# Two of TensorE's transpositions handed to DMA, and the opening's transfers in another order

## What is computed

```python
for l in range(DEPTH):                                   # 2 layers
    x = x + 0.5 * swiglu(rms_norm(x, ...), w_ffn1_in[l], w_ffn1_out[l])
    x = x + hybrid_mixer(rms_norm(x, ...), mem, ...)
    x = x + 0.5 * swiglu(rms_norm(x, ...), w_ffn2_in[l], w_ffn2_out[l])

# hybrid_mixer: four branches of width 512 over h, gated and summed
proj = h @ w_in
o_a = moba_attention(...)              # 8 heads of 64, rotary; causal softmax (one block of 256)
o_b = multiscale_pool(...)             # four running means, mixed by four 128x128 matrices
o_c = forgetting_attention(...)        # "fox": 8 heads of 64, causal softmax with a decay term
o_m = memory_cross_attention(...)      # 4 heads of 128; keys and values from mem
y = einsum('bsnc,ncd->bsnd', stack(o_a, o_b, o_c, o_m), w_branch)
return sum(sigmoid(gate_logits) * y) @ w_out
```

## Time and profile before

| | |
|---|---|
| Median of 3 runs | 1331.98 us (1331.53 to 1332.44) |
| The profiled execution's own time | 1332.22 us |
| Its span | 1330.3 us |
| PE busy | 1324.3 us, 100% of the span |
| DVE busy | 930.7 us, 70% |
| ACT busy | 681.0 us, 51% |
| POOL busy | 260.8 us, 20% |
| DMA, mean | 200 GB/s |

### The profile page before, as it was taken

The page is one execution under the profiler, slowest core; times in us unless marked ns, Lnnn a source line. Parts: engine busy times, 40 slices in busy tenths (PEclk is TensorE's granted clock), DMA queues, the critical chain, the costliest instruction groups (busy, mean ns, idle before and its releaser), DMA issues.

```text
span 1330.3 us, 15825 instructions
## 1 busy us (share of the span) xinstructions
PE 1324.3 (100%) x6140; PEld 1095.3 (82%) x6140; DVE 930.7 (70%) x1182; ACT 681.0 (51%) x952; POOL 260.8 (20%) x257
## 2 busy tenths in 40 slices
PE   9999999999999999999999999999999999999999
PEld 7888888888888888888888888888888888888887
DVE  5666777789897675666475664787999876665653
ACT  5444465554655455454355454556546545544442
POOL 0323312033120002333003230020522100033220
PEclk9999999999999999999999999999999999999999
DMA  8877566568554547776557675555665645477671
GB/s 312 245 231 220 163 233 203 194 174 269 175 175 158 190 129 253 211 229 214 190 190 222 207 228 191 196 164 182 210 222 174 205 159 190 164 222 223 213 214 64
DMA packets 192698, 266.34 MB, mean 200 GB/s; under 512 B 81504, under 2 KB 91248, under 8 KB 192624
## 3 DMA queue, kind: packets, MB, share of 16 engines
q1 hardware_dynamic: 191408, 261.84, 62.4%
q0 software_dynamic: 928, 3.17, 0.7%
q10 hardware_dynamic: 288, 0.33, 0.1%
HBM read 245.37 MB, written 1.06 MB: 185 GB/s over the span
## 4 chain that ended last, share of the span: by engine, by line
PE 97%; DVE 2%; ACT 0%; DMA 0%; issue 0%; SPq 0%; ACTq 0%; DVEq 0%
PE psum L678 24%; PE psum L938 22%; PE psum L705 21%; PE psum L686 12%; PE psum L943 11%; PE psum L896 1%; PE psum L815 1%; PE psum L799 1%; PE psum L834 1%; PE psum L900 1%; PE psum L804 1%; DVE ring_lo L1409 0%; PE psum L633 0%; PE psum L843 0%; DMA x<-in_x 0%; PE psum L881 0%
## 5 line engine op out<-in xcount | busy, mean ns | idle before, releaser
L1409 DVE TENSOR_TENSOR ring_lo<-raw,ring_hi 128x1024 fp32r<-128x1024 f32 x459 | 594.7, 1310 | 318.5 <-ACT ring_hi L1009 316.7
L1009 ACT ACTIVATE ring_hi<-raw 128x1024 fp32r<-128x1024 f32 x463 | 481.2, 1048 | 566.1 <-PE psum L686 235.9
L678 PE MATMUL psum<-ring_hi,hT 128*128 128x512 f32 x1408 | 348.2, 390 | 0.2 <-DVE ring_hi L1849 0.2
L678 PEld LDWEIGHTS psum<-ring_hi,hT 128*128 128x128 f32 x1408 | 264.4, 188 | 55.1 <-DVE ring_hi L1849 0.5
L938 PE MATMUL psum<-ring_hi,hT 128*128 128x512 f32 x960 | 240.7, 393 | 0.0
L938 PEld LDWEIGHTS psum<-ring_hi,hT 128*128 128x128 f32 x960 | 178.3, 188 | 38.1 <-ACT ring_hi L1009 0.7
L686 PE MATMUL psum<-ring_lo,hT 128*128 128x512 f32 x704 | 188.6, 390 | 0.0
L1310 POOL COPY planes<-gate 128x1024 uint16<-128x1024 uint16 (+1 forms) x48 | 67.9, 1444 | 534.2 <-DVE gate L1483 534.2
L686 PEld LDWEIGHTS psum<-ring_lo,hT 128*128 128x128 f32 x704 | 132.0, 188 | 27.2
L943 PE MATMUL psum<-ring_lo,hT 128*128 128x512 f32 x480 | 128.4, 390 | 0.0
L705 PE MATMUL psum<-ring_hi,act_hi 128*128 128x512 f32 x352 | 110.5, 390 | 0.0
(11 more groups left out here) (194 smaller groups left out, 1154.6 us busy)
## 6 DMA issues: line engine op xcount, KB each, us to landing
raw<-in_w_ffn_in SPq DMA_DIRECT2D x78, 1024.0 KB, 5.2
raw<-in_w_in SPq DMA_DIRECT2D x64, 1024.0 KB, 5.2
raw<-in_w_ffn_out SPq DMA_DIRECT2D x44, 1024.0 KB, 5.0
raw<-in_w_branch SPq DMA_DIRECT2D x16, 1024.0 KB, 5.1
raw<-in_w_ffn_in SPq DMA_DIRECT2D x19, 512.0 KB, 5.0
raw<-in_w_mem_kv SPq DMA_DIRECT2D x8, 1024.0 KB, 5.2
raw<-in_w_out SPq DMA_DIRECT2D x8, 1024.0 KB, 4.9
forget<-negc_rows POOLq DMA_DIRECT2D x2, 1024.0 KB, 7.8
```

The lines of the kernel that those rows point to most:

```text
L678: pe.matmul(outs[t][:, :], hT[part][:, kc, t * P:(t + 1) * P], w[0][:, kc - first, :], start=kc == 0 and part == 0, stop=False)
L1009: act.activation(unit_out(0, step, k), view, ACT.Copy).then_inc(hi_done.sem, 1)
L1409: dve.tensor_tensor(unit_out(1, step, k), view, unit_out(0, step, k).bitcast(F32), ALU.subtract)\
```

## The change

Three things are changed. (1) The memory queries: POOL parts them, SP issues a DMA transposition behind the load of `gate(1,1).0`, POOL merges, and ACT scales the merged columns in place; PE's eight transpositions go. (2) The probabilities of group 4: ACT parts them in `y(0,0)`, SP issues two DMA transpositions behind the load of `y(2,0)`, POOL merges them in six copies, PE's twelve transpositions go, and its values stand three steps later, at the end of `y(0,1)`. (3) The opening: the gains are issued by ACT, the first weight rows by SP behind the first half of x, and DVE rounds these rows after three columns instead of four.

```diff
-        ("PE", _step_of("gate", (1, 0), 1), END, 0), ("ACT", _step_of("gate", (1, 0), 1), END, 0),
+        ("ACT", _step_of("gate", (1, 0), 1), END, 0),
...
-ROWS_BEHIND = {_step_of("qm", None, 1): 0, _step_of("qc"): 1, ...
+ROWS_BEHIND = {_step_of("qm", None, 1): 0, _step_of("gate", (1, 1)): 1, _step_of("qc"): 2, ...
...
-BY_DMA, BY_PE = (0, 1), (2, 3, 4, 5)
+BY_DMA, BY_PLANES, BY_PE = (0, 1), (4,), (2, 3, 5)
+PLANES_BEHIND = {_step_of("y", (2, 0)): 4}
...
-    (4, _step_of("gate", (0, 0)), _step_of("gate", (0, 0), 1), _step_of("y", (0, 0)), _step_of("gate", (0, 1))),
+    (4, _step_of("gate", (0, 0)), _step_of("gate", (0, 0), 1), None, _step_of("y", (0, 1))),
...
+    if g in BY_PLANES:
+        TASKS.setdefault(("ACT", exps + 1, MIDDLE), []).append(("planes", g))
...
                 load_x(0)
-                sp.dma_start(raw_unit(0, 0)[:, 1:2, :], rows(1, 1)).then_inc(first_rows[1], 16)
+                for kc in range(2):
+                    sp.dma_start(raw_unit(0, 0)[:, kc:kc + 1, :], rows(kc, 1)).then_inc(first_rows[kc], 16)
...
+                    if m in PLANES_BEHIND:
+                        g = PLANES_BEHIND[m]
+                        sp.wait_ge(head_planes.sem, ...)
+                        for h in range(2):
+                            sp.dma_start_transpose(planes_out(g)[h]..., pT_flat.bitcast(U16)[:, 1536 * h:1536 * (h + 1)]).then_inc(head_turned.sem, 16)
...
 # PE, values
+                    elif arg in BY_PLANES:
+                        pe.wait_ge(head_merged.sem, ...)
+                        pe.wait_ge(max_ready.sem, max_ready.at(L, arg + 2))
...
 # ACT, qkT
-                    if arg == MEM:
-                        act.wait_ge(qkT_ps.sem, qkT_ps.at(L, 1))
...
+                    job, at = (QM_ROWS, 2) if arg == MEM else (QC_ROWS, 0)
+                    act.wait_ge(rows_merged.sem, rows_merged.at(L, job + 1))
+                    columns = qkT_buf[:, arg % 2, 0]
+                    act.activation(columns, columns, ACT.Copy, scale=gain(L, HEAD_AT + at)).then_inc(qT_ready[arg].sem, 1)
...
+                elif stage == "planes":
+                    act.wait_ge(pv_ready.sem, pv_ready.at(L, arg))
+                    act.wait_ge(probs_ready.sem, probs_ready.at(L, arg + 1))
+                    for h in range(2):
+                        last = act.activation(pT_flat.bitcast(U16)[:, 1536 * h:1536 * (h + 1)], halves_of(probs[:, None, :])[:, h, 0, :], ACT.Copy)
+                    last.then_inc(head_planes.sem, 1)
...
-            act.dma_start(first_piece(None, 0), w1i_d[0, 0:P, 0:GROUP]).then_inc(first_rows[0], 16)
+            act.dma_start(gains[:, 0, 0:KC], gains_d[:, 0, 0:KC]).then_inc(first_gains, 16)
...
 # POOL
-            pool.dma_start(gains[:, 0, 0:KC], gains_d[:, 0, 0:KC]).then_inc(first_gains, 16)
...
                 turn_rows(L, KMEM_ROWS, kmem[:, :, :], qkT_buf[:, MEM % 2, 1])
+                pool.wait_ge(taken_dve.sem, taken_dve.at(L, release("qm")))
+                turn_rows(L, QM_ROWS, qk[:, 0], qkT_buf[:, MEM % 2, 0])
                 turned(L, 0)
...
+                merged(L, 4)
...
 # DVE, opening
-            first_columns(0)
+            first_columns(range(3))
             dve.wait_ge(first_rows[0], 16)
             dve.tensor_copy(first_piece(0, 0), first_piece(None, 0)).then_inc(first_hi, 1)
+            first_columns(range(3, 4))
```

More of the change, by code:

```diff
@@ L409, in plane_words @@
             return NT * 512
-        KMEM_ROWS, QA_ROWS, QC_ROWS, KC_ROWS = range(4)
+        KMEM_ROWS, QM_ROWS, QA_ROWS, QC_ROWS, KC_ROWS = range(5)
         def row_planes(job):
@@ L422, in planes_of, with planes_out @@
             return pT_flat[:, 0:plane_words(g)].bitcast(U16)
+        def planes_out(g):
+            homes = [kmem[:, :, :], qkT_buf[:, FOX % 2, 1]] if g // 2 == MOBA else [qkT_buf[:, MOBA % 2, i] for i in range(2)]
+            return [words.rearrange("p t c -> p (t c)")[:, 0:768].bitcast(U16) for words in homes]
         def first_bank(kc):
@@ L771, in task @@
                 elif stage == "qkT":
-                    if arg == MOBA:
-                        pe.wait_ge(rotated.sem, rotated.at(L, 2))
-                    if arg == MEM:
[L776 to L780, removed]
+                    pe.wait_ge(rotated.sem, rotated.at(L, 2))
+                    attended(L, 2)
                     for c in range(BC):
@@ L790, in task @@
                     if arg >= 2:
-                        attended(L, arg)
+                        attended(L, arg - 1 if arg - 1 in BY_PLANES else arg)
                     if arg:
@@ L1186, in task @@
                     last.then_inc(exp_done.sem, 1)
+                elif stage == "planes":
+                    act.wait_ge(pv_ready.sem, pv_ready.at(L, arg))
+                    act.wait_ge(probs_ready.sem, probs_ready.at(L, arg + 1))
+                    for h in range(2):
+                        last = act.activation(pT_flat.bitcast(U16)[:, 1536 * h:1536 * (h + 1)],
+                                              halves_of(probs[:, None, :])[:, h, 0, :], ACT.Copy)
+                    last.then_inc(head_planes.sem, 1)
                 elif stage == "probsT":
@@ L1367, in turn_rows, with merged @@
                 return last
+            def merged(L, g):
+                at = BY_PLANES.index(g)
+                pool.wait_ge(head_turned.sem, head_turned.at(L, 32 * (at + 1)))
+                for h in range(2):
+                    blocks = planes_out(g)[h].rearrange("p (odd q s) -> p odd q s", odd=2, q=6)
+                    for b, block_of in ((0, slice(0, 2)), (1, slice(2, 6, 2)), (2, slice(3, 6, 2))):
+                        words = pT[:, b, :].bitcast(U16).rearrange("p (j odd s h) -> p h odd j s", j=2, odd=2, h=2)
+                        last = pool.tensor_copy(words[:, h], blocks[:, :, block_of, :])
+                last.then_inc(head_merged.sem, 1)
             for L in range(DEPTH):
@@ L1836, in first_remainder, with first_columns @@
                 return dve.tensor_tensor(first_piece(1, kc), first_piece(None, kc), first_piece(0, kc).bitcast(F32), ALU.subtract)
-            def first_columns(half):
-                for kc in range(4 * half, 4 * half + 4):
+            def first_columns(chunks):
+                for kc in chunks:
                     dve.wait_ge(columns_hi, kc + 1)
@@ L1852, in _ @@
             lo(0, 0, 1)
-            first_columns(1)
+            first_columns(range(4, 8))
             dve.sem_inc(h_ready.sem, 4)
```

41 lines of the change are left out of this document (21 added, 20 removed).

## The result

The changed kernel takes 1343.7 us (median of 4 runs, 1343.45 to 1345.25); the kernel before took 1331.76 beside it (4 runs, 1331.49 to 1332.44). The ratio is 1.0091, 95% interval 1.0074 to 1.0109: slower by 0.9%, 11.9 us. The forecast was 1346.5 in a range of 1337 to 1356.

What follows compares the result with a forecast made beforehand. PE was taken to bound the kernel, busy for the whole span. Per layer +6.1 + 1.8 + 1.0 - 1.36 = +7.5, two layers +15.1, opening -0.5: +14.6 on 1332.2, given as 1346.5 us, range 1337 to 1356.

Steps and rivals of the forecast that it cites:

- PE is the bound, and a wait is never given back: Whole span: PE is always busy, so work taken from it shortens the time and any wait on it lengthens it.
- The queries' wait: Group 0's scores: the chain through POOL, SP, POOL and ACT ends at 268.5 instead of 262.36, 6.1 us net per layer.
- The clock: Behind PE's stall at the scores: the clock falls to half, costing 1.8 us per stall, bounds 0 and 3.7.
- The rival that the clock holds: Behind the stall at the scores: the stall comes but the clock stays up, total 1343; chance 20%.
- Group 4: Group 4's values: planes merged at about 425 when PE asks at 424.1, 1.0 us late per layer, bounds 0 and 5.
- The rival with 4 to 5 us: Group 4's values: transpositions directly behind a load land late, 4 to 5 us per layer instead of 1, total 1354; chance 17%.
- The transpositions taken off: PE's eight transpositions of queries and twelve of probabilities: 0.92 and 1.36 us off per layer, 4.6 us in two layers.
- The opening: Start of the kernel: DVE's rounding one column earlier lets PE start sooner, 0.5 us off, bounds 1.0 off and 0.4 on.

Runs made afterwards that it cites:

- run 9: Changed kernel with the queries' transposition ahead of its load, group 0's scores at the end of `qa.0`, group 4 as in run 8: 1327.56 us, ratio 0.9966.
- run 2: Kernel before with only the memory queries turned by DMA; group 4 on PE, old opening: 1349.04 us, ratio 1.0128.
- run 4: Changed kernel with the memory queries back on PE, so opening and group 4 only: 1331.36 us, ratio 0.9992 against the kernel before.
- run 10: Changed kernel with group 4 as in run 8 and 29 products of the identity in PE's wait for the queries: 1339.83 us, ratio 1.0059.
- run 12: Kernel before with nine products of zeros instead of seven while x comes: 1331.98 us, ratio 0.9999.
- run 3: Kernel before with only group 4's new way: 1332.65 us, ratio 1.0002.
- run 7: Changed kernel with ACT's scaling and the scores of group 0 moved behind `y(1,0)`: 1335.67 us, ratio 1.0024 against the kernel before.
- run 5: Changed kernel with 22 products of the identity, result unread, in front of group 0's scores: 1345.25 us, ratio 1.0097 against the kernel before.
- run 8: Kernel of run 4 with group 4's transpositions issued ahead of the load of `y(2,0)`, behind that of `gate(2,0).1`: 1327.49 us, ratio 0.9966.
- run 1: Kernel before with the opening's change alone: 1330.44 us, ratio 0.9989.
- run 11: Kernel before with the opening's new transfers, but DVE's first rows behind four columns as before: 1330.96 us, ratio 0.9991.
- run 6: Changed kernel with SP's transposition of the memory queries ahead of the load of `gate(1,1).0`: 1343.41 us, ratio 1.0082 against the kernel before.

## Why the prediction was right

- **PE is the bound, and a wait is never given back.** Right but for some tenths: the losses and gains above add to the span's 11.7 us. Where PE runs ahead, small waits on DVE's shares eat up to 0.9 us of a gain (run 9).
- **The queries' wait.** Forecast 6.1 us net per layer, measured 5.98 and 5.72. Link by link 4.0, 6.4, 3.2, 1.2 stood against 3.94, 6.68, 2.75, 1.15. This is the step that decided the sign, and runs 2 and 4 show that it alone does. The median landing, 6.4, happened to fit a place 0.9 us behind a load; 0.41 us behind one it would have been 7 us or more.
- **The clock.** The fall was right, its size was not. 1.8 us were taken, between bounds of 0 and 3.7, for 3.6 us of slow work; measured are 2.40 and 2.13 by the offsets and 2.3 and 2.0 by run 10. PE worked at half clock for about 4.7 us in layer 0 (266.56 to 271.2) and 4.1 in layer 1 (932.74 to 936.8), half of which is the loss. That 1.8 came so near is partly luck: the 3.6 us were read from the opening of one trace, and run 12 shows that this stretch differs from trace to trace without the pause deciding it; over all profiled waits of 5.8 to 6.7 us the loss is 1.8 to 2.8. The rival that the clock holds is refuted by the windows. The total couldn't have done it: that rival's 1343 lies nearer to the measured 1343.7 than the forecast's 1346.5, because the opening and group 4 came out 3 us better. The Trainium skill, "TensorE: Matmul & The Clock Gate", Part 1, says that idleness puts the array back to half of its clock. The trace agrees: 0.50 from 266 to 270. Behind short pauses the traces show both: 2.14 us was followed by 0.50 in run 3 and not in run 4, 2.45 in one layer of run 7 and not in the other.
- **Group 4.** Forecast 1.0 us late per layer, measured 0.2 and at most 0.05: the term was mis-sized, mainly by the landing, 8.1 us where 9.0 were taken (410.4 to 419.4). The rival with 4 to 5 us didn't come, but its mechanism exists: in runs 3, 4 and 5 the same code was 2.1 us late in one layer, by a landing of 9.6 us.
- **The transpositions taken off.** 1.36 us forecast for twelve, 1.40 and 1.33 by run 8. For the eight 0.92 forecast, and PE does reach its wait 0.93 and 0.91 us sooner.
- **The opening.** Forecast -0.5 with bounds of -1.0 and +0.4, measured -1.77, and -1.6 by run 1: the one term that missed its own bounds. The prediction named x's second piece, which no longer goes beside 256 KB of weights, and left it nearly unpriced: 0.4 of its 0.5 was DVE's column. Run 11 puts 1.2 us on the transfers.

The errors: opening -1.3, group 4 -1.7, clock +0.9, queries -0.5, the shares of group 2 -0.3; together -2.9, from the forecast's +14.6 to the measured +11.7.

The price of the queries differs with what stands beside them. Against run 8, where group 4 never waits, the changed kernel is 16.2 us longer, about the 8.37 + 7.85 of the sum above. Against run 4 it is only 12.3, because run 4 has group 4's waits of 2.4 us, and in seven of eleven executions the half clock behind them, where the changed kernel has 0.25 us. By themselves (run 2) they cost 17.0 by the medians and 16.4 in the layers of the profiled execution.

What stays open: why group 4's pair lands after some 8 us in both layers of the changed kernel but after 9.6 in one layer of runs 3, 4 and 5, at the same distance of 0.41 us behind its load; and what decides whether the clock falls behind a pause of 2 to 3 us, and how long it stays down.

## What to carry to other kernels

Work handed from a busy engine to a chain of idle ones is bought with latency: add the links (here 4 + 6.7 + 2.8 + 1.2 us for eight transpositions of 0.9) and compare with the distance to the consumer before counting what is saved; if the distance is too short, move the consumer, or leave the work where it is. A DMA that something waits for goes onto its queue ahead of a large load, not directly behind it: one changed entry turned a part that brought nothing (run 3) into one of 2.9 us (run 8 against run 1). And a pause of a saturated TensorE can cost more than its length: behind the pauses of 5.8 us and more in these runs it always did, behind those of 2.1 to 2.9 us at times, behind one of 1.7 us it didn't. So shortening a long pause by 1 us brought 0.3 us, and closing it brought the clock back too.

## What the runs showed of the hardware

**A DMA transposition behind a load.** Over all runs the time from issue to landing goes with the distance to the load in front on the same queue: 7.0 to 8.7 us for a single one issued 0.41 us behind it, mostly 6.3 to 6.7 at 0.9 us (some 7.1 to 8.3), mostly 4.9 to 5.3 at 1.9 us, mostly 4.2 to 5.5 at 4 us or more. Runs 6 and 8 changed only the place in the queue, so there it is cause and not only company. The spread of the earlier trace rows is mostly this.

**POOL and DVE slow each other.** The same four merging copies took 2.75 us while DVE waited, and 4.00, 4.13 and, in run 9, 6.31 beside its work. In the changed kernel DVE's remainders, two at a time, beside POOL's parting and without POOL:

```profile
251.78 3.19 DVE L1439 TENSOR_TENSOR ring_lo<-raw,ring_hi 128x1024 fp32r<-128x1024 f32 x2
...
418.75 2.35 DVE L1439 TENSOR_TENSOR ring_lo<-raw,ring_hi 128x1024 fp32r<-128x1024 f32 x2
```

This is why shortening one link of the chain lengthened the next one (run 6). The Trainium skill, "SBUF — State Buffer", section "Who interferes with whom", describes a pair of ports that DVE and GpSimd share, an instruction of one holding it while the other waits. The trace agrees that the two cost each other time, 3.19 us against 2.35 on DVE's side; which instruction held what, no run here shows.

**The price of filler.** A float32 product of the identity, 128x128, costs PE 0.23 us (29 in 6.64 us), more than twice a float32 transposition of the same size (twelve in 1.23 us). The profile counts two matmuls for each product (58 for 29) and one for each transposition.
